# Attention scores of both heads of a pair in one block of matmuls, head by head in turn

## What is computed

```python
z = jnp.einsum('bhqd,bhkd->bhqk', q_blk.astype(jnp.float32), k32) * scale
mask = key_pos[None, :] < q_pos[:, None]
log_1m_beta = jnp.where(mask, jax.nn.log_sigmoid(-z), 0.0)
stick = lax.cumsum(log_1m_beta, axis=3, reverse=True) - log_1m_beta
att = jnp.where(mask, jnp.exp(jax.nn.log_sigmoid(z) + stick), 0.0)
return jnp.einsum('bhqk,bhkd->bhqd', att, v32)
```

## Time and profile before

| | |
|---|---|
| median of 3 runs | 1756.73 us (1755.76 to 1756.87) |
| profiled execution | 1754.75 us, of which the span is 1753.0 us |
| TensorE busy in the span | 1709.8 us (98%) |
| DVE, ACT, POOL busy | 1292.4, 771.7, 767.4 us |
| matmuls of the scores (L289) | 64 records, all between 35.1 and 191.5 us |

### The profile page before, as it was taken

One profiled execution on the slowest core, in us unless ns is written; L12 is line 12 of the kernel. 1 busy time (PEld: TensorE's weight loads), 2 busy tenths in 40 slices (PEclk: granted clock), 3 DMA queues, 4 the chain that ended last, 5 costly groups with the idle time before them and its releaser, 6 DMA issues.

```text
span 1753.0 us, 24582 instructions
## 1 busy us (share of the span) xinstructions
PE 1709.8 (98%) x9066; PEld 1519.8 (87%) x9066; DVE 1292.4 (74%) x1844; ACT 771.7 (44%) x1092; POOL 767.4 (44%) x486
## 2 busy tenths in 40 slices
PE   7999999998999999999999999999999999999997
PEld 5778778887889999999999999999888888888885
DVE  2555511115999899989999789886787787787786
ACT  5444433234333566746667466654223323323322
POOL 3332334332311455665666578881533333332330
PEclk9999999999999999999999999999999999999998
DMA  5222223322235777777777988888999999999992
GB/s 156 73 60 84 60 73 95 108 73 72 84 118 191 221 247 247 240 251 283 259 248 254 327 306 299 292 305 318 376 370 377 360 346 378 361 357 360 368 343 103
DMA packets 212293, 413.80 MB, mean 236 GB/s; under 512 B 11504, under 2 KB 150800, under 8 KB 206864
## 3 DMA queue, kind: packets, MB, share of 16 engines
q1 hardware_dynamic: 156880, 253.78, 41.8%
q0 software_dynamic: 36864, 134.23, 21.4%
q10 hardware_dynamic: 18496, 25.19, 4.1%
HBM read 360.73 MB, written 52.43 MB: 236 GB/s over the span
## 4 chain that ended last, share of the span: by engine, by line
PE 80%; DVE 10%; POOL 3%; DMA 2%; ACT 2%; issue 2%; ACTq 0%; SPq 0%; DVEq 0%; POOLq 0%
PE psum L1205 28%; PE psum L229 22%; PE psum L1146 21%; PE psum L1136 4%; DVE ring L1468 2%; DVE ul L1393 2%; PE psum L1173 2%; DMA ring<-in_expert_u,index 1%; PE psum L303 1%; PE psum L289 1%; POOL ring L1352 1%; POOL grid L1371 1%; PE psum L423 1%; PE psum L317 1%; DVE hot L1456 1%
## 5 line engine op out<-in xcount | busy, mean ns | idle before, releaser
L1146 PE MATMUL psum<-xTh,uh 128*128 128x384 f32 x1024 | 354.1, 346 | 9.8 <-DVE ul L1393 9.3
L1146 PE MATMUL psum<-xTl,uh 128*128 128x384 f32 x1024 | 343.3, 335 | 0.0
L1146 PE MATMUL psum<-xTh,ul 128*128 128x384 f32 x1024 | 343.3, 335 | 0.0
L1352 POOL DMA_INDIRECT ring<-in_expert_v,index x128 | 176.9, 1382 | 311.0 <-DVE acc L1473 269.0
L212 POOL TENSOR_TENSOR wl<-raw,wh 128x1024 fp32r<-128x1024 f32 x72 | 172.5, 2403 | 320.9 <-ACT wh L485 320.9
L1205 PE MATMUL psum<-vh,dwh 128*128 128x512 f32 x768 | 298.8, 389 | 1.2 <-DVE dwl L1486 1.2
L1205 PE MATMUL psum<-vl,dwh 128*128 128x512 f32 x768 | 298.8, 389 | 0.0
L1205 PE MATMUL psum<-vh,dwl 128*128 128x512 f32 x768 | 298.8, 389 | 0.0
L1278 ACT ACTIVATE vh<-v_raw 128x4096 fp32r<-128x4096 f32 x31 | 112.6, 3634 | 340.2 <-PE psum L1205 339.8
L1352 POOL DMA_INDIRECT ring<-in_expert_u,index x128 | 172.9, 1351 | 152.6 <-DVE ring L1468 80.1
L1468 DVE SCALAR_TENSOR_TENSOR ring<-ring,x 128x1024 f32<-128x1024 f32 x120 | 199.8, 1678 | 12.3 <-DMA ring<-in_expert_u,index 11.0
(11 more groups left out here) (206 smaller groups left out, 2893.3 us busy)
## 6 DMA issues: line engine op xcount, KB each, us to landing
u_raw<-in_expert_u SPq DMA_DIRECT2D x128, 512.0 KB, 4.5
v_raw<-in_expert_v SPq DMA_DIRECT2D x30, 2048.0 KB, 12.2
expert_act<-hb ACTq DMA_DIRECT2D x128, 192.0 KB, 3.9
expert_gate<-grid SPq DMA_DIRECT2D x12, 2048.0 KB, 7.2
dh<-expert_act SPq DMA_DIRECT2D x32, 768.0 KB, 4.4
dg<-expert_gate SPq DMA_DIRECT2D x32, 768.0 KB, 6.7
raw<-in_w_in SPq DMA_DIRECT2D x40, 512.0 KB, 3.8
raw<-in_w_q SPq DMA_DIRECT2D x16, 512.0 KB, 4.0
```

What stands on the lines that cost most here:

```text
L1146: last = nc.tensor.matmul(zb[s][:, 0:DT], w[s][:, c, :], x[:, c, 0:DT], start=(c == 0 and i == 0), stop=(c == C - 1 and i == 2))
L1352: nc.gpsimd.indirect_dma_start(out=ring[k][:], out_offset=None, in_=tables[x // SLOTS], in_offset=bass.IndirectOffsetOnAxis(ap=index[:, x ...
```

## The change

TensorE's `scores` now computes both heads: block by block, first head 0, then head 1. Head 0's blocks stay in `zt`; head 1's go to `pj[2]`, `tp` and `pj[1]`, banks which the value and key projections and the value transposes use. So the block waits also for `taken[2]` (and for `v_ready` of the pair before), `transpose_v` waits until both heads are copied, and ScalarE copies both heads one after the other, ahead of the cb tile.

```diff
+    SCORE_AT = ({0: (zt[0], 0), 1: (zt[1], 0), 3: (zt[1], 3 * P), 2: (zt[2], 0)},
+                {0: (pj[2], 0), 1: (tp, 0), 3: (tp, 3 * P), 2: (pj[1], 0)})
...
-        def scores(p, e):
+        def scores(p):
 
             pe.wait_ge(taken[1], p * 2 + 1)
-
-            if e == 0:
-                pe.wait_ge(S["t_used"], p * 2 + PRIMED)
-            else:
-                pe.wait_ge(S["z_copied"], p * 2 + 1)
-            h = slice(e * HD, (e + 1) * HD)
-            for kb, o in ROW.items():
-                last = nc.tensor.matmul(zt[o // T][:, o % T:o % T + T - kb * P], kT[h, kb * P:(kb + 1) * P],
-                                        qT[h, kb * P:], start=True, stop=True)
+            pe.wait_ge(taken[2], p * 2 + 1)
+            pe.wait_ge(S["t_used"], p * 2 + PRIMED)
+            if not isinstance(p, int):
+                pe.wait_ge(S["v_ready"], p)
+            for kb in (0, 1, 3, 2):
+                n = T - kb * P
+                for e in range(2):
+                    h = slice(e * HD, (e + 1) * HD)
+                    bank, at = SCORE_AT[e][kb]
+                    last = nc.tensor.matmul(bank[:, at:at + n], kT[h, kb * P:(kb + 1) * P], qT[h, kb * P:], start=True, stop=True)
             last.then_inc(S["z_full"], 1)
...
-            scores(p, 0)
+            scores(p)
             project(0, r + 1, xh, xl)
+            pe.wait_ge(S["z_copied"], p * 2 + 2)
             transpose_v(p)
-            scores(p, 1)
             project(1, r + 1, xh, xl)
...
         def copy_scores(p, e):
-            act.wait_ge(S["z_full"], p * 2 + e + 1)
+            act.wait_ge(S["z_full"], p + 1)
             for b, n in enumerate((T, T, ZW - 2 * T)):
-                last = nc.scalar.activation(z[:, e, b * T:b * T + n], zt[b][:, 0:n], ACT.Copy)
+                bank, at = SCORE_AT[e][(0, 1, 2)[b]]
+                last = nc.scalar.activation(z[:, e, b * T:b * T + n], bank[:, at:at + n], ACT.Copy)
...
             copy_scores(p, 0)
+            copy_scores(p, 1)
             take(0, r + 1, cb[:])
             high(0, r + 2)
             softplus(p, 0)
-            copy_scores(p, 1)
             softplus_hi(p, 0)
```

## The result

The changed kernel took 1747.22 us (median of 6 runs, 1745.53 to 1752.2) against 1756.8 us for the kernel before in the same runs (6 runs, 1754.36 to 1761.3): a ratio of 0.9949, 95% interval 0.9934 to 0.9964. The 95% interval leaves room for 6 to 12 us, so the medians alone do not say what the change is worth; the chains do. The profiled execution took 1746.34 us, its span is 1744.6.

What follows compares the result with a forecast made beforehand. TensorE's chain, busy 98% of the span, was taken to bound the kernel; 3 x 2.35 - 4e - 0.75 + 0.25 with e = 0.3 gains 5.35 us, giving 1751.4 us, range 1748.0 to 1755.5.

Steps and rivals of the forecast that it cites:

- I take e = 0.3: Scores block: e is what head 1 still adds to the 2.35 us of a block, taken as 0.3 us.
- 0.22 us is the cost of getting in and out: Scores of one head: 2.35 us less 2.13 us of columns leaves 0.22 us for entering and leaving the block.
- the block that goes: TensorE's separate head-1 scores block: its removal shortens the stretch from first scores to first sums by 2.35 us.
- So of the 2.35 us pair 3 keeps 0.25 us: Pair 3's masked adds: GpSimd's weight split comes between VectorE's two, so only 0.25 us of the gain stays.
- if L740 in pair 3 stays at 0.84: Sign of a wrong prediction: pair 3's two masked adds were to take 2.9 us in place of 0.84.
- Rival 1: Pair 3 keeps its gain, the second masked add preceding GpSimd's turn: 2.1 us more, 1749.3 us; chance 0.17.
- The wait for `taken[2]`: Pair 0's scores must wait for ScalarE's vT copy: costs 0.75 us once, 0 in pairs 1 to 3.
- The wait for the copies: Before the value transposes: both heads' copies take 2.7 us beside a projection of 5.67, so cost 0.
- the moved second copy: ScalarE's copy of head 1's scores stays where it was, measured from the end of the scores: cost 0.
- the arguments of head 0: VectorE's work after the first sums: begins no earlier, since the convolution's last step ends there; cost 0 in the loop.
- second sums: TensorE asks at 116.22, the arguments' PSUM reads are done at 114.70: 1.5 us to spare, cost 0 in the loop.
- Rivals 2 to 4: Scores blocks: weak overlap, 1753.0 to 1755.0 us (0.12); no overlap, 1758.7 (0.13); slower, array emptied at changes, 1764.9 (0.06).

Runs made afterwards that it cites:

- the first experiment: The changed kernel with both heads' score matmuls fed from rows 0 to 63, head 0's scores computed twice: 1753.84 us, ratio to the kernel before 0.999.

## Why the prediction was wrong

By its own steps:

- *What bounds, and where the change acts.* Right: it is TensorE's chain through the pairs, and 4 x 2.56 - 0.75 = 9.49 of the 9.51 us between the two marks come from there.
- *"I take e = 0.3".* Mis-sized. Head 1 adds 2.36 - 2.35 = 0.01 us (0.08 in pair 0). The two reasons for e > 0 both took weight loads to pass one at a time, every 0.10 us. They do not. The changed kernel's weight loads at the start of pair 1's block, in order of time:

```profile
79.86 0.30 PEld L294 LDWEIGHTS psum<-qT,kT 64*128 64x128 f32 x4 [0.17 <-issue]
```

  Four loads in 0.30 us, where one head's two took 0.29: the other row half's go beside them. Four times 0.29 us too little.
- *"0.22 us is the cost of getting in and out", and the block that goes is worth "2.35 us".* Mis-sized. The removed block was worth 2.35 + 0.22 = 2.57. The three projections that followed it now follow the transposes, and take 16.37 us and not 16.59: a group behind scores pays 0.22 us at its start, outside the group of scores. I read it as the price of leaving the row halves; no run separates it from other reasons. I had the whole cost inside the 2.35. Four times 0.22 us too little.
- *"So of the 2.35 us pair 3 keeps 0.25 us".* This step failed and was the largest single error, 2.1 us: pair 3 kept the whole gain. From the end of its first scores to the first gated projection it was 224.35 - 180.71 = 43.64 us and is 213.57 - 172.58 = 40.99. The mechanism is real: it appears in full with one matmul more, at the place and price forecast (2.92 us for the two adds in place of 0.77), and goes when the split goes. But I placed the first masked add 35.32 us behind the scores' end and it came at 207.68 - 172.58 = 35.10, because of those same 0.22 us. The split came at 208.09 - 172.58 = 35.51, as forecast, and by then VectorE had been in its second add for 0.07 us. The prediction's own sign of being wrong, "if L740 in pair 3 stays at 0.84", is this one. Rival 1, "the 0.2 us between them fall otherwise", is what happened, and its 0.17 was too little for a margin of 0.2 us, taken from a sum whose terms were no better than that. That it came out on the good side is luck.
- *The wait for `taken[2]`.* Right: 0.75 us, once, undone without remainder.
- *The wait for the copies, the moved second copy, the arguments of head 0, second sums.* Right at cost 0: between pairs nothing but TensorE is in the chain.
- *Rivals 2 to 4* fell with the first experiment: 4.51 us with one row half, 2.36 with two, and no gap at the turns.

With the measured values the sum is 4 x 2.56 - 0.75 = 9.5 us, 1745.3 us against the profiled execution of before and 1747.2 against its median of 1756.73. That the median is met so closely is partly luck, since executions of one kernel differ by several us. The errors are 2.1, 1.16 and 0.88 us, 4.1 in all, the difference between 5.35 and 9.49. The range failed because all three had one sign and two of them one cause, the 0.22 us.

## What to carry to other kernels

Matmuls that use only half of the array's rows or columns should stand in turn with those of the other half, into other banks or partitions: two heads then cost what one does, and head-by-head order gives three quarters of that away. When a stream that bounds the kernel is shortened, ask at its next wait what the others do at that moment; where the answer turns on 0.1 or 0.2 us, carry both outcomes in the range, or move the colliding instruction. And small work that runs in TensorE's idle stretch can be worth keeping there: in the one profiled execution without it the granted clock fell.

## What the runs showed of the hardware

- Weight loads of one row half do not hold up those of the other: four in 0.30 us, two of one half in 0.29.
- TensorE does not always start matmuls in program order. The first one of the other half passed exactly three that had not begun, for row halves (in the run with head 0 first) and for column halves (the outputs of the kernel before) alike.
- VectorE's and GpSimd's instructions of the kind above exclude each other one by one: of two VectorE instructions in a row, the second goes on at once if GpSimd has not yet asked (0.77 us for the two), and waits for the whole 2.4 us split if it has (2.92 us). 0.22 us decide over 2.15. In the experts, where GpSimd was first, VectorE's step took 2.61 us and not 1.24.
- In one execution, after 3.8 us without any work for TensorE, the granted clock stood at 0.50, and the outputs took 4.55 us in place of 2.3. With 2.7 us of matmuls in that stretch it stayed at 1.00.
- Behind a block of scores the next projection takes 5.67 us, behind the transposes three take 16.37 (5.46 each).
